# One-core decoder step: the last expert pass added through a one-hot table, row loads in freed buffers, the shared product spread over pairs

## The chip, the cores and the metric

The kernel runs on one core of a Trainium2 chip. The metric is the device time of one launch in microseconds (us). Engines are named as the profile names them: PE (matrix), DVE (vector), ACT (scalar), POOL (GpSimd) and SP (which only starts DMAs here).

## What is computed

One decoder layer for 576 tokens (512 prompt tokens, 64 sample tokens): attention and a gated convolution, a layer norm, a mixture of 64 experts, a shared expert, a per-layer embedding term, a second layer norm. What the change touches is the second half:

```python
eidx, gw = route(x2, lw['w_router'], lw['router_bias'])      # 6 of 64 experts a token
ffn = (swiglu(x2, lw['w_s_gate'], lw['w_s_up'], lw['w_s_down'])          # shared expert
       + routed_experts(x2, eidx, gw, lw['w_e_gate'], lw['w_e_up'], lw['w_e_down']))
ple = jax.nn.sigmoid(h @ lw['w_ple_gate']) * (p @ lw['w_ple_proj'])
h = layer_norm(DN_ALPHA * h + ffn.reshape(n, s, D_MODEL) + ple, lw['ln2_g'], lw['ln2_b'])
```

A token is 1024 wide, an expert's hidden width is 256, everything is float32. An expert's three matrices are 3 MB, so 64 experts are about 200 MB to be read.

## The kernel before

**Passes and pairs.** Experts are taken in 32 pairs (`pair(p, i)`). A pair's weights (six loads of 1 MB: gate, up and down of both experts) go into one of three buffers, `w_exp[RING[p % 3]]`, at the SBUF offsets `o_w0`, `o_w1` and `o_w2`. A pass computes 64 rows of each of the two experts. A pair takes as many passes as its fuller expert needs, read at run time from `n_pass`. In this input there are 40 passes; the running sum after each pair is in `cum_pass`, and if it came out odd the last pair would get an empty pass more.

**What each engine does in a pass k.** PE multiplies the turned rows `xt` by gate (`gate_mm`) and up (`gu_ready`), transposes the next pass's rows (`turn`, L1311), transposes the hidden rows, and multiplies by down (`y_mm`). ACT and DVE scale the two halves of the result by the token's weight into `ysb[:, k % 2]`. POOL gathers the rows of pass k + 2 from DRAM into `xg` (L690) and then scatters `ysb` to `expert_rows` in DRAM (L715), one row for each of a token's six choices. Both are indirect DMAs on POOL's queue; all three streams use the same 16 DMA engines.

**What SP does.** It loads pair p (`next_pair`, L569) part by part. Each part waits for the same part of pair p - 3 to have been used and for that of pair p - 1 to have landed. The weights of pair 2 and, ahead of them, the shared expert's down matrix `w_sdn` (L610) wait until PE has finished the last of 20 units of the embedding gate (`u_ready`). PE turns the rows of pass 0 just ahead of that unit.

**The shared expert's down product** (`shared_down`, `shared_add`) is ten tiles of 512 columns, put behind pairs 0, 1 and 2 as `SD_AFTER` says (4, 3 and 3 tiles). Behind each group PE waits until DVE has added the last of them.

**The last stage.** When all passes are scattered, POOL signals `all_out` and SP loads the rows back, nine loads of 1.5 MB: two for each of the four prompt tiles (`part[t]`, L623), one for the sample tile (`fold`, L625). For a prompt tile PE sums the first `N_ON_PE[t]` of the six rows through the identity matrix (L1401), DVE adds the others to `res` (`add_rows`, L1939), then the sum of PE (`add_sum`, L1955), ACT makes the variance (L970), DVE scales (`last_norm`, L1966 and L1968) and SP writes the tile out (L630). The sample tile comes last and is folded by DVE and PE.

## Time and profile before

| | |
|---|---|
| median of 3 runs | 1310.81 us (1310.05 to 1314.06) |
| time of the profiled execution | 1311.96 us |
| its span in the profile | 1310.1 us |
| PE busy | 1223.2 us, 93% of the span |
| DVE busy | 488.2 us, 37% |
| ACT, POOL busy | 304.2 us and 159.5 us |
| HBM read, written | 295.95 MB and 26.94 MB |

The profile lists when instructions ran on each engine and what the engine had waited for. DMA shares are the busy part of 16 DMA engines; they can read a little over 1. Times of single instructions are counted from the start of the span.

### The profile page before, as it was taken

How to read it: one execution, taken by the hardware profiler on the slowest of the kernel's cores; microseconds unless marked ns; L12 is line 12 of the kernel's file. 1: busy time of each engine (PE TensorE's matmuls, PEld its weight loads, DVE VectorE, ACT ScalarE, POOL GpSimd, SP SyncE). 2: the span in 40 equal slices, each digit the busy share in tenths (PEclk: the TensorE clock that was granted, in tenths of full speed). 3: DMA queues.
4: the chain of work that ended last, by engine and by line, in shares of the span. 5: the costliest groups of instructions: out<-in, count | busy, mean ns of one | idle time of the engine just before them, and what ended most of it. 6: DMA issues, size and time to landing. Idle time of an engine off the chain costs nothing.

```text
span 1310.1 us, 23451 instructions
## 1 busy us (share of the span) xinstructions
PE 1223.2 (93%) x8835; PEld 988.2 (75%) x8836; DVE 488.2 (37%) x1072; ACT 304.2 (23%) x557; POOL 159.5 (12%) x230
## 2 busy tenths in 40 slices
PE   6999999999999999999998899999998899999745
PEld 6988879999999999998996556666665566666412
DVE  4355683423344334575872221111111111111137
ACT  3254553312122223124121011111111111111102
POOL 0200000000000000006152111121121111211100
PEclk9999999999999999999999999999999999999968
DMA  9311212232323232433519998999999999999785
GB/s 270 102 33 65 65 34 65 65 97 65 97 66 98 65 114 81 153 95 126 225 47 413 420 393 328 419 421 422 420 412 411 415 413 408 415 408 418 295 318 231
DMA packets 101263, 308.08 MB, mean 235 GB/s; under 512 B 11435, under 2 KB 62467, under 8 KB 76613
## 3 DMA queue, kind: packets, MB, share of 16 engines
q1 hardware_dynamic: 87636, 275.20, 54.8%
q0 software_dynamic: 12480, 28.60, 5.7%
q10 hardware_dynamic: 1088, 3.47, 0.8%
q8 instruction: 41, 0.67, 0.2%
q14 instruction: 18, 0.14, 0.0%
HBM read 295.95 MB, written 26.94 MB: 246 GB/s over the span
## 4 chain that ended last, share of the span: by engine, by line
PE 51%; DMA 38%; DVE 5%; issue 1%; SPq 1%; DVEq 1%; ACT 1%; POOL 1%; ACTq 0%; POOLq 0%
DMA w_exp<-in_w_e_down_dram 35%; PE proj L992 31%; PE proj L1172 4%; PE att L1349 2%; PE proj L1366 2%; PE proj L1301 2%; DMA part<-expert_rows 2%; PE att L1097 1%; PE att L1059 1%; PE att L1181 1%; PE proj L1025 1%; SPq L623 1%; PE att L1172 1%; PE att L1110 1%; PE att L1381 1%
## 5 line engine op out<-in xcount | busy, mean ns | idle before, releaser
L1349 PE MATMUL att<-w_exp,xt 128*64 128x256 f32 x2560 | 288.9, 383 | 21.6 <-issue 10.0
L1349 PEld LDWEIGHTS att<-w_exp,xt 128*64 128x64 f32 x2560 | 221.1, 138 | 99.6 <-issue 46.6
L992 PE MATMUL proj<-h_hi,w_hi 128*128 128x288 f32 x768 | 171.2, 304 | 0.0
L992 PE MATMUL proj<-h_hi,w_lo 128*128 128x288 f32 x768 | 164.2, 295 | 0.0
L992 PE MATMUL proj<-h_lo,w_hi 128*128 128x288 f32 x768 | 164.0, 295 | 0.0
L1366 PE MATMUL proj<-w_exp,ht_e 128*64 128x512 f32 x640 | 147.3, 601 | 9.3 <-issue 5.2
L992 PEld LDWEIGHTS proj<-h_hi,w_hi 128*128 128x128 f32 x768 | 122.0, 189 | 16.2 <-issue 15.2
L992 PEld LDWEIGHTS proj<-h_lo,w_hi 128*128 128x128 f32 x768 | 123.6, 189 | 0.0
L992 PEld LDWEIGHTS proj<-h_hi,w_lo 128*128 128x128 f32 x768 | 123.4, 188 | 0.0
L448 DVE TENSOR_TENSOR w_lo<-w_raw,w_hi 128x2048 fp32r<-128x2048 f32 x33 | 75.6, 2290 | 94.4 <-ACT w_hi L438 88.1
L1366 PEld LDWEIGHTS proj<-w_exp,ht_e 128*64 128x64 f32 x640 | 50.5, 137 | 78.6 <-issue 75.8
L438 ACT ACTIVATE w_hi<-w_raw 128x2048 fp32r<-128x2048 f32 x33 | 63.0, 1910 | 90.6 <-PE proj L992 73.9
L1911 DVE TENSOR_SCALAR ysb<-proj,tabw 128x512 f32 x40 | 30.0, 751 | 140.3 <-PE proj L1366 140.3
L1902 DVE TENSOR_TENSOR sg<-sg,att 128x256 f32<-128x256 f32 x40 | 16.8, 421 | 127.5 <-ACT sg L947 127.5
L1906 DVE TENSOR_TENSOR h_e<-sg,att 128x256 f32<-128x256 f32 x40 | 16.8, 421 | 123.6 <-PE att L1349 123.6
L954 ACT ACTIVATE ysb<-proj,tabw 128x512 f32 x40 | 27.5, 687 | 141.8 <-PE proj L1366 141.8
L1311 PEld LDWEIGHTS proj<-ident,xg 128*128 128x128 f32 x328 | 43.5, 195 | 19.7 <-issue 15.1
L949 ACT ACTIVATE ht_e<-att 128x256 f32<-128x256 f32 x40 | 15.3, 383 | 185.3 <-PE att L1355 185.3
L1311 PE MATMUL proj<-ident,xg 128*128 128x128 f32 x328 | 54.5, 290 | 4.0 <-DMA xg<-x_rows,gidx_col 4.0
L715 POOL DMA_INDIRECT expert_rows<-ysb,sidx_col x40 | 40.4, 1010 | 137.8 <-DVE ysb L1911 133.5
L992 PE MATMUL proj<-mix_hi,w_lo 128*128 128x288 f32 x256 | 54.8, 296 | 0.0
L992 PE MATMUL proj<-mix_hi,w_hi 128*128 128x288 f32 x256 | 54.8, 296 | 0.0
(342 smaller groups left out, 1761.0 us busy)
## 6 DMA issues: line engine op xcount, KB each, us to landing
w_exp<-in_w_e_gate_dram SPq DMA_DIRECT2D x64, 1024.0 KB
w_exp<-in_w_e_up_dram SPq DMA_DIRECT2D x64, 1024.0 KB
w_exp<-in_w_e_down_dram SPq DMA_DIRECT2D x64, 1024.0 KB
w_raw<-in_w_in_dram SPq DMA_DIRECT2D x21, 1024.0 KB
part<-expert_rows SPq DMA_DIRECT2D x8, 1536.0 KB, 17.8
w_raw<-in_w_in_dram SPq DMA_DIRECT2D x8, 512.0 KB
w_raw<-in_w_attn_out_dram SPq DMA_DIRECT2D x8, 512.0 KB
w_raw<-in_w_conv_out_dram SPq DMA_DIRECT2D x4, 1024.0 KB
```

The source lines that it names most:

```text
L438: nc.scalar.activation(w_hi[:, g.par, :], w_raw[:, g.par, :], ACT.Copy).then_inc(hi_done, 1)
L448: nc.vector.tensor_tensor(w_lo[:, g.par, :], w_raw[:, g.par, :], w_hi[:, g.par, :].bitcast(F32), ALU.subtract).then_inc(w_ready, 1)
L715: pool.indirect_dma_start(out=rows_d[:, :], out_offset=bass.IndirectOffsetOnAxis(ap=sidx_col[i][:, 0:1], axis=0), in_=ysb[:, i, :], in_off ...
L954: nc.scalar.activation(ysb[:, bass.ds(side_of, 1), 0:512].rearrange("p o n -> p (o n)"), proj[:, 2, :], ACT.Copy, scale=tabw[:, bass.ds(k, ...
L992: last = nc.tensor.matmul(proj[:, 2 * i + a, 0:HALF], lhs, x[:, c, a * HALF:(a + 1) * HALF], start=(c == 0 and n == 0), stop=(c == KC - 1 ...
L1172: last = nc.tensor.matmul(out, x[:, c, t * P:t * P + w], v[:, c, :], start=(c == 0 and n == 0), stop=(c == KC - 1 and n == 2))
L1301: last = nc.tensor.matmul(gate_bank(u)[0:w, :], x[:, c, t * P:t * P + w], v[:, c, :], start=(c == 0 and n == 0), stop=(c == KC - 1 and n = ...
L1311: last = nc.tensor.transpose(proj[:, half, c * P:(c + 1) * P], xg[:, :, half * 4 + c], ident[:, :])
L1349: last = nc.tensor.matmul(att[e * SLOT:(e + 1) * SLOT, m, 0:FF], xt[:, c, e * SLOT:(e + 1) * SLOT], weights[e][:, c, :], start=(c == 0), s ...
L1366: last = nc.tensor.matmul(proj[e * SLOT:(e + 1) * SLOT, 2 + half, :], ht_e[:, c, e * SLOT:(e + 1) * SLOT], down[e][:, c, half * 512:(half ...
L1902: nc.vector.tensor_tensor(sg[:, :], sg[:, :], att[:, 0, 0:FF], ALU.mult)
L1911: nc.vector.tensor_scalar(ysb[:, bass.ds(side_of, 1), 512:D].rearrange("p o n -> p (o n)"), proj[:, 3, :], tabw[:, bass.ds(k, 1)], None, A ...
```

## The change

Five things change.

1. **Last pass.** The last pass is no longer scattered to DRAM and read back. POOL's loop makes one pass fewer (`half_all` is one lower, one `next_rows` stands behind the loop). Its results stay in `ysb[:, 1]`. ACT and DVE split them into `y_hi` and `y_lo`, and PE adds them to each token tile's sum through `slot_hot`, a table with a one where slot and token match, made by DVE behind pair 19. As its rows in `expert_rows` are still read, POOL writes zeros there from the cleared `xg`, ahead of the first gather, which waits for it.
2. **Row loads.** The row tiles now lie in the three weight buffers: four loads in `o_w2`, four in `o_w0`, one in `o_w1`. `all_out` comes when pass 38 is scattered, and SP starts each group of loads when the pair that last used the buffer is done (`pair_done`). A row tile is 3 x 1024 floats in one piece. The sample tile comes second, and PE sums its three pieces itself (`fold_rows` is gone).
3. **Shared product.** One tile behind each of pairs 5 to 14 (`SD_FIRST`, `N_SD`), in one PSUM bank. `w_sdn` is loaded behind the weights of pair 4.
4. **Gain and bias of the second norm.** ACT loads one row of each ahead of the passes, where before it loaded them spread over 128 partitions behind the passes; PE spreads them through a row of ones behind pairs 15 to 18, DVE copies them.
5. **Code.** 20 pairs are written out for PE and DVE (before 5 and 3) and the rest looped; ACT has one loop. `N_ON_PE` of tile 3 is 3 instead of 4. ACT reads its square-root table ahead of the tiles.

```diff
+SD_FIRST = 5
+N_SD = 2 * NT
+N_UNROLLED = 20
+LAST_ORDER = (0, NT - 1, *range(1, NT - 1))
-N_ON_PE = (2, 3, 4, 4)
+N_ON_PE = (2, 3, 4, 3)
...
+        o_part = [(o_w2, o_w0, o_w1)[n // 4] + n % 4 * 12 * D for n in range(9)]
...
-            sp.dma_start(w_sdn[:, :, :], w_sd[0].rearrange("(c p) n -> p c n", p=P)).then_inc(sd_in, 16)
             load_parts(2, 2, range(4))
             sp.wait_ge(res_done, 1)
             load_parts(2, 2, range(4, 6))
             for p in range(3, 5):
                 next_pair(p, RING[p % 3], p - 3)
+            sp.dma_start(w_sdn[:, :, :], w_sd[0].rearrange("(c p) n -> p c n", p=P)).then_inc(sd_in, 16)
...
             sp.wait_ge(all_out, 1)
...
+            def pair_done(p):
+
+                done = sp.value_load(cum_pass[0:1, p:p + 1], min_val=1, max_val=MAXPASS - 1)
+                sp.wait_ge(y_mm, done)
+                past(nc.sync, 4)
...
+            pair_done(NPE - 3)
+            for h in range(2):
+                load_rows(0, h)
...
+            load_rows(1, 0)
+            pair_done(NPE - 2)
+            load_rows(1, 1)
+            for h in range(2):
+                load_rows(2, h)
+            load_rows(3, 0)
+            pair_done(NPE - 1)
+            load_rows(3, 1)
...
-            gather(0, 0, 1)
+            k_half = half_passes(pool)
+            nc.gpsimd.tensor_copy(sidx_col[1][:, :], tabs[:, bass.ds(k_half * 2 + 1, 1)]).then_inc(idx_ready, 1)
+            pool.wait_ge(idx_ready, 1)
+            pool.indirect_dma_start(out=rows_d[:, :], out_offset=bass.IndirectOffsetOnAxis(ap=sidx_col[1][:, 0:1], axis=0),
+                                    in_=xg[:, :, :].rearrange("p q c -> p (q c)"), in_offset=None, bounds_check=8 * T - 1,
+                                    oob_is_err=False).then_inc(scattered, 16)
+            pool.wait_ge(scattered, 16)
+            gather(0, 0, 2)
...
             with pool.Fori(0, k_half) as it:
...
+                    next_rows(it * 2 + i, i)
+            next_rows(k_half * 2, 0)
...
+            act.wait_ge(y_a, k + 1)
+            act.wait_ge(y_dv, k + 1)
+            past(nc.scalar, 0)
+            nc.scalar.activation(y_hi[:, :], ysb[:, 1, :], ACT.Copy).then_inc(y_hi_ready, 1)
+            nc.scalar.activation(sink_s[:, :], eps[:, :], ACT.Sqrt)
...
-            for p in range(5):
+            for p in range(N_UNROLLED):
                 pair(p, RING[p % 3])
...
+                if 0 <= n < N_SD:
+                    shared_down(n)
+                if N_SD <= n < N_SD + 4:
+                    spread_row(n)
...
+            for s, t in enumerate(LAST_ORDER):
+                w = ntok(t)
+                if s == 4:
+                    pe.wait_ge(part_added, 1)
+                out = sum_banks(s)[0:w, :, :]
...
+                pe.wait_ge(y_lo_ready, 1)
                 for half in range(2):
...
+                    for n, y in enumerate((y_hi, y_lo)):
+                        last = nc.tensor.matmul(out[:, half, :], slot_hot[:, t * P:t * P + w],
+                                                y[:, half * 512:(half + 1) * 512], start=False, stop=(n == 1))
...
+            dve.wait_ge(y_hi_ready, 1)
+            dve.drain()
+            nc.vector.tensor_tensor(y_lo[:, :], ysb[:, 1, :], y_hi[:, :].bitcast(F32), ALU.subtract).then_inc(y_lo_ready, 1)
...
+            for s in range(NT + 2):
+                if s < NT and LAST_ORDER[s] < NT - 1:
+                    add_rows(LAST_ORDER[s])
+                if 1 <= s <= NT:
+                    add_sum(s - 1, LAST_ORDER[s - 1])
+                if s >= 2:
+                    last_norm(s - 2, LAST_ORDER[s - 2])
```

On POOL, at the end of the embedding units, the first gather stood like this before (`xg` are the gathered rows, `ppo` the embedding product, `xtr` PE's signal that rows are turned):

```order
L661 TENSOR_TENSOR ppo_131<-ppo_131,sig_g 64x256 [waits u_sig]
L687 COPY gidx_col_201<-tabx 128x1 [waits x_zero,x2_out,routed]
L690 DMA xg<-x_rows,gidx_col_201 128x1024 [waits idx_ready]
L661 TENSOR_TENSOR ppo_131<-ppo_131,sig_g 128x256 [waits u_sig] x4
L661 TENSOR_TENSOR ppo_131<-ppo_131,sig_g 64x256 [waits u_sig]
```

In the changed kernel the same place on POOL reads:

```order
L690 TENSOR_TENSOR ppo_131<-ppo_131,sig_g 64x256 [waits u_sig]
L474 TENSOR_LOAD half_all [waits x_zero,x2_out,routed]
L474 ISA x2
L724 ISA
L724 COPY sidx_col_204<-tabs 128x1
L726 DMA expert_rows<-xg,sidx_col_204 4608x1024 [waits idx_ready]
L716 COPY gidx_col_201<-tabx 128x1 [waits scattered]
L719 DMA xg<-x_rows,gidx_col_201 128x1024 [waits idx_ready]
L690 TENSOR_TENSOR ppo_131<-ppo_131,sig_g 128x256 [waits u_sig] x4
```

The write of zeros, and the wait for its landing, have come between the embedding products and the first gather, and the last five products stand behind both.

On SP, behind the loop over pairs, the end of the program was this:

```order
L623 DMA part_205<-expert_rows 128x3x1024 [waits all_out]
L623 DMA part_205<-expert_rows 128x3x1024
L623 DMA part_206<-expert_rows 128x3x1024 x2
L623 DMA part_207<-expert_rows 128x3x1024 x2
L623 DMA part_208<-expert_rows 128x3x1024 x2
L625 DMA fold<-expert_rows 128x3x1024
```

In the changed kernel it is this, still on SP:

```order
L635 TENSOR_LOAD cum_pass [waits all_out]
L635 ISA x2
L642 DMA part_0_205<-expert_rows 128x3072 [waits y_mm]
L642 DMA part_1_206<-expert_rows 128x3072
L648 DMA fold<-expert_rows 128x3072
L642 DMA part_0_207<-expert_rows 128x3072
...
L642 DMA part_1_208<-expert_rows 128x3072 [waits y_mm]
L642 DMA part_0_209<-expert_rows 128x3072
L642 DMA part_1_210<-expert_rows 128x3072
L642 DMA part_0_211<-expert_rows 128x3072
...
L642 DMA part_1_212<-expert_rows 128x3072 [waits y_mm]
```

There are still nine loads, and `all_out` is still ahead of them; only the last one waits for the last pair.

## Rows read from the trace of the kernel before

**Rows 1.** The page: span, and DMA busy share in 40 slices.

```profile
span 1310.1 us, 23451 instructions
DMA  9311212232323232433519998999999999999785
```

**Rows 2.** Stretches: busy us of each engine (instructions), PE clock, DMA share, GB/s.

```profile
700.00:770.00 70.00, 59.37 (x338) 33.47 (x338) 14.25 (x24) 6.53 (x13) 9.22 (x15) 0.98 1.01 414
770.00:797.60 27.60, 27.23 (x212) 18.44 (x209) 4.84 (x9) 4.48 (x9) 4.84 (x8) 1.00 0.78 303
797.60:1236.00 438.40, 417.13 (x3054) 274.07 (x3050) 77.39 (x136) 69.34 (x135) 82.70 (x136) 0.99 1.01 412
1236.00:1254.06 18.06, 8.92 (x59) 5.18 (x58) 2.28 (x4) 2.05 (x4) 2.43 (x4) 0.88 0.33 113
1254.06:1290.40 36.34, 23.06 (x42) 9.54 (x43) 19.52 (x21) 4.35 (x7) 0.00 (x0) 0.73 0.99 394
```

**Rows 3.** Timeline of PE behind pair 2: start, us, what ran [idle before].

```profile
768.54 7.13 PE L1349 MATMUL att<-w_exp,xt 128*64 128x256 f32 x64 [1.96 <-issue]
780.89 7.10 PE L1349 MATMUL att<-w_exp,xt 128*64 128x256 f32 x64
```

**Rows 4.** Instructions grouped by line, pair stage: count, busy us, mean ns.

```profile
L1381 PE MATMUL att<-w_sdn,hs_x 128*128 128x512 f32 (+1 forms) x40 | 18.1, 601 | 0.0
```

**Rows 5.** Timeline of SP: the loads around the dip in DMA.

```profile
701.57 0.38 SPq L610 DMA_DIRECT2D w_sdn<-in_w_s_down_dram  x1
781.32 0.84 SPq L569 DMA_DIRECT2D w_exp<-in_w_e_down_dram  x2
797.63 0.99 SPq L569 DMA_DIRECT2D w_exp<-in_w_e_gate_dram  x2
```

**Rows 6.** Timeline of POOL and PE: first gather; a scatter and the gather behind it.

```profile
688.10 1.35 POOL L690 DMA_INDIRECT xg<-x_rows,gidx_col  x1 [0.95 <-POOL gidx_col L687]
697.67 1.13 PE L1311 MATMUL proj<-ident,xg 128*128 128x128 f32 x8 [0.72 <-DMA xg<-x_rows,gidx_col]
...
807.80 1.00 POOL L715 DMA_INDIRECT expert_rows<-ysb,sidx_col  x1 [3.38 <-DVE ysb L1911]
...
815.54 1.04 POOL L690 DMA_INDIRECT xg<-x_rows,gidx_col  x1 [0.85 <-DMA expert_rows<-ysb,sidx_col]
```

**Rows 7.** Who waited for whom, pair stage: us in total, times, longest.

```profile
PE att L1349 <- DMA w_exp<-in_w_e_up_dram: 9.7, 5, 2.5
```

**Rows 8.** Timeline: the last two scatters, and the start of the row loads.

```profile
1232.76 1.02 POOL L715 DMA_INDIRECT expert_rows<-ysb,sidx_col  x1 [4.03 <-DVE ysb L1911]
...
1248.84 1.01 POOL L715 DMA_INDIRECT expert_rows<-ysb,sidx_col  x1 [4.04 <-DVE ysb L1911]
1254.06 15.81 SPq L623 DMA_DIRECT2D part<-expert_rows  x8
```

**Rows 9.** Timeline of DVE: rows of tiles 0 and 3 added, last instruction.

```profile
1264.13 5.13 DVE L1939 TENSOR_TENSOR res<-res,part 128x1024 f32<-128x1024 f32 x4 [16.27 <-DMA part<-expert_rows]
...
1287.03 2.53 DVE L1939 TENSOR_TENSOR res<-res,part 128x1024 f32<-128x1024 f32 x2 [0.78 <-DMA part<-expert_rows]
...
1305.50 1.28 DVE L1968 SCALAR_TENSOR_TENSOR res<-res,rstd,g2b 64x1024 f32<-64x1024 f32 x1
```

**Rows 10.** Instructions grouped by line, last stage.

```profile
L1401 PE MATMUL att<-part,ident 128*128 128x512 f32 x32 | 15.7, 654 | 2.2 <-DMA part<-expert_rows 2.2
L1939 DVE TENSOR_TENSOR res<-res,part 128x1024 f32<-128x1024 f32 x11 | 13.5, 1226 | 22.4 <-DMA part<-expert_rows 21.9
L1968 DVE SCALAR_TENSOR_TENSOR res<-res,rstd,g2b 128x1024 f32<-128x1024 f32 (+1 forms) x5 | 6.4, 1283 | 0.4
L1966 DVE SCALAR_TENSOR_TENSOR res<-res,mv,g2b 128x1024 f32<-128x1024 f32 (+1 forms) x5 | 6.3, 1263 | 0.0
```

**Rows 11.** Single microseconds of the last stage, columns as in Rows 2.

```profile
1250.00:1251.00 1.00, 0.00 (x0) 0.00 (x0) 0.00 (x0) 0.00 (x0) 0.00 (x0) 0.50 0.94 258
1282.00:1283.00 1.00, 1.00 (x3) 0.41 (x2) 0.89 (x2) 0.00 (x0) 0.00 (x0) 0.50 1.03 418
```

More of the change, by code:

```diff
@@ L1386, in _, with shared_down, spread_row @@
-            for p in range(5):
+            def shared_down(n):
+                t, c = QUADS[n]
+                w = ntok(t)
+                pe.wait_ge(sd_read, n)
+                for k in range(2):
+                    last = nc.tensor.matmul(sd_bank(n)[0:w, :], hs_x[:, k, t * P:t * P + w],
+                                            w_sdn[:, k, c * 512:(c + 1) * 512], start=(k == 0), stop=(k == 1))
+                last.then_inc(sd_ready, 1)
+            def spread_row(n):
+                i, c = divmod(n - N_SD, 2)
+                pe.wait_ge(sd_read, n)
+                nc.tensor.matmul(sd_bank(n), ones_row[:, :], g2b2[0:1, i, c * 512:(c + 1) * 512],
+                                 start=True, stop=True).then_inc(sd_ready, 1)
@@ new lines, in _ @@
+            with pe.Fori(0, (NPE - N_UNROLLED) // 3) as it:
+                for i in range(3):
+                    pair(it * 3 + (N_UNROLLED + i), RING[(N_UNROLLED + i) % 3])
+            k = pe.snap(count, min_val=0, max_val=MAXPASS - 2)
+            pe.wait_ge(y_a, k + 1)
+            pe.wait_ge(y_dv, k + 1)
+            past(nc.tensor, 1)
+            pe.wait_ge(hot_ready, 1)
+            for s, t in enumerate(LAST_ORDER):
+                w = ntok(t)
+                if s == 4:
+                    pe.wait_ge(part_added, 1)
+                out = sum_banks(s)[0:w, :, :]
+                if t == NT - 1:
+                    pe.wait_ge(part_in[t], 16)
+                    for half in range(2):
+                        for j in range(TOPK // 2):
+                            nc.tensor.matmul(out[:, half, :], fold_id[:, :], fold[:, j, half * 512:(half + 1) * 512],
+                                             start=(j == 0), stop=False)
+                else:
+                    pe.wait_ge(part_in[t], 32)
+                    for half in range(2):
+                        for j in range(N_ON_PE[t]):
+                            nc.tensor.matmul(out[:, half, :], ident[:, :], part_row(t, j, half), start=(j == 0), stop=False)
+                pe.wait_ge(y_lo_ready, 1)
@@ L1403, in _ @@
                 last.then_inc(part_sum, 1)
-            pe.wait_ge(folded, 1)
-            pe.wait_ge(part_added, 1)
-            for half in range(2):
-                last = nc.tensor.matmul(sum_banks(NT - 1)[0:NS, half, :], fold_id[:, :],
-                                        fold[:, 0, half * 512:(half + 1) * 512], start=True, stop=True)
-            last.then_inc(part_sum, 1)
         @block.vector
@@ L1934, in add_rows @@
+            dve.drain().then_inc(hot_ready, 1)
+            with dve.Fori(0, NPE - N_UNROLLED) as it:
+                passes(it + N_UNROLLED)
+            dve.wait_ge(y_hi_ready, 1)
+            dve.drain()
+            nc.vector.tensor_tensor(y_lo[:, :], ysb[:, 1, :], y_hi[:, :].bitcast(F32), ALU.subtract).then_inc(y_lo_ready, 1)
             def add_rows(t):
```

187 lines of the change are left out of this document (86 added, 101 removed).

## The prediction, made blind

> **What bounds the kernel now.** I read the page first: from about 690 us on, the DMA share is nine tenths or more in nearly every slice [rows 1]. That is the pair stage, 200 MB of weights. A table of stretches then says where the transfers stand still. Between 700 and 770 us and again from 797.6 to 1236 us the share is 1.01, which is as full as this trace reads [rows 2]. It drops twice: to 0.78 in the 27.6 us from 770 on, and to 0.33 in the 18 us between the last weights and the first row load [rows 2]. From 1254.06 on it is full again with the row loads, and then a tail of DVE and output follows to the end.
>
> So two kinds of time can be gained: idle DMA inside the pair stage, and time around its end. PE work in the pair stage is worth something only where it keeps a buffer from coming free.
>
> The first dip is such a place. SP issues the down part of one pair at 781.32 and the next gate part at 797.63 [rows 5]: it waits for a buffer. PE runs its passes back to back there, 12.35 us apart (768.54 and 780.89) [rows 3], and it is late because of the shared product: 18.1 us of matmuls [rows 4], and behind each of the three groups a gap of 1.9 to 2.0 us in which PE waits for DVE (one of the three: [rows 3]). Between two pairs without a shared group there is no gap [rows 3]. Later PE waits for weights: 9.7 us for up parts alone, five times [rows 7].
>
> **1. Start of the pair stage: a loss.** Before, POOL issued the first gather at 688.10, and PE, which waited for it, turned the rows at 697.67: 9.6 us, beside weight loads that fill the queues [rows 6]. Now POOL first loads a register, copies an index, writes the zeros and waits until they have landed, and the gather queues behind all that. PE's last gate unit stands behind the turn, SP's loads of pair 2 behind that unit, and with them every later load.
> - The register load has no row of its own. The 1.96 us gap contains one, beside other work [rows 3], so it costs 0 to 2 us; I take 1.0.
> - An indirect write in a full queue: issued at 807.80, and the gather of 815.54, which had 0.85 us of idle before it, is put down to its landing [rows 6]. So it landed 6.9 to 7.7 us after its issue; I take 7.3. Below, the last scatter, in a nearly empty queue, took at most 5.2 us to the row loads (1248.84 to 1254.06) [rows 8]. Above, 9.6 as the gather.
> - Index copy and its wait again: 1.3 us (0.95 of it the wait) [rows 6].
> - The gather now runs while the queue drains: between 5.2 (as above) and 9.6; I take 7.0.
>
> Sum 1.0 + 7.3 + 1.3 + 7.0 = 16.6 against 9.6: PE's turn and SP's loads come 7.0 us later. Bounds: with 5.2 twice and no register load +2.1, with 9.6 twice and 2 us +12.9.
>
> The Trainium skill (DMA: Bandwidth & Descriptors, section Anatomy of one DMA) fits a POOL-issued DMA with 2.0 us plus its bytes at 436 GB/s. By it each of the two 0.5 MB transfers would take 3.2 us (an estimate), the start would be about 1 us earlier than before, and the sum below 1290.5. The trace disagrees while SP's queue is full: 9.6 us for the gather.
>
> **2. The dip: a gain.** PE reaches pair 3 earlier by 18.1 us and three gaps of 1.9, together 23.8, less the 7.0. The gate part of 797.63 could then be issued some 17 us earlier, and the dip is only (1.01 - 0.78) / 1.01 x 27.6 = 6.3 us of idle DMA, so all of it goes. In exchange the queue is empty for the 7.0 us at the start. `w_sdn` is only moved. The zeros are new traffic: 0.5 MB at 0.414 MB/us is 1.3 us at most. The longer code for PE (15 more pairs written out) adds bytes I take as nothing.
>
> Last weights: +7.0 - 6.3 + 1.3 = 2.0 us later. Bounds: -3 and +8.
>
> PE must not become the bound instead. The ten tiles come back behind pairs 5 to 14 (18.1 us), and four spread rows of at most half a tile each (0.9) make 3.6. So by pair 18 PE stands at +7.0 - 23.8 + 18.1 + 3.6 = 5 us later than before, and it has 9.7 us of waits for weights to give there [rows 7]. Hidden. DVE's table behind pair 19 (some 12 small instructions) lies in DVE's idle time: DVE is busy 77 of 438 us [rows 2].
>
> **3. The row loads: the main gain.** `all_out` now needs the scatter of pass 38, issued at 1232.76, instead of that of pass 39, issued at 1248.84 [rows 8]. From there to SP's first load it took 5.2 us before; weights still land until about 1236 [rows 2], so I take 6.0, and 1.0 for SP's register load. With the 2.0 us of part 2: 1232.8 + 2.0 + 6.0 + 1.0 = 1241.8, which is 12.3 us ahead of 1254.06. The buffers are no limit: eight of the nine loads need pairs 29 and 30, whose last pass is 38, and the ninth pair 31, done before its turn in the queue comes.
>
> The loads themselves take as long as before. The first two land 10.1 us after the first issue (1254.06 to 1264.13), the eighth 33.0 us after (1287.03) [rows 8, 9]: 3.8 us each. The order is tile 0, samples, 1, 2, 3, so tile 3 is complete with the ninth load, 10.1 + 7 x 3.8 = 36.7 us after the issue: 1278.5. Pieces of 12 KB instead of 4 KB I count as nothing: the share is already 0.99 [rows 2].
>
> **4. The end behind the last rows.** DVE has, behind tile 3's rows: three adds (1.23 each and their drains, 3.8), the sum of tile 2 (1.22 and two small ones, 1.4), the norm of tile 1 (1.26 + 1.28 + 0.2 = 2.7), the sum of tile 3 (1.4), the norms of tiles 2 and 3 (5.5) (means of each line: [rows 10]): 14.8 us, to 1293.3. The output took 1310.1 - 1306.8 = 3.3 us behind DVE's last instruction [rows 9, 1]. That gives a span of 1296.6.
>
> Does PE keep up? A tile is six matmuls of two records, 12 x 0.43 = 5.2 us at the full clock (15.7 us for 32 records, low stretch included, is 0.49 [rows 10]), and four one-hot matmuls, at most one record each, 1 to 2 us: 6.2 to 7.2 against 7.6 us of loading. Tile 2 has eight, and ends about 1279.5, tile 3 about 1285.5; DVE asks for it at 1286.5. So PE is hidden by 1 us. `y_hi` and `y_lo`, one instruction each of about the 1.23 us of a row add [rows 10], are made while the first rows are on their way.
>
> Other edits count as nothing: the two 0.5 MB loads of gain and bias ran while SP waited; the table load of ACT lay behind tile 0, not at the end.
>
> **Sum.** Span 1310.1 - 13.5 = 1296.6; the profiled execution's time was 1311.96, so 1298.5 by its own. That execution lies 1.2 us above the median of the three runs, 1310.81, from which the same sum gives 1297.3. I say 1298.
>
> **Rivals.**
> - *Start hidden.* Both indirect transfers take 5.2 us and the register load nothing: a delay of 2.1, the last weights 2.9 us sooner than before and 4.9 sooner than in my sum: 1293. For it: without pair 2's loads the queue runs dry while the gather is under way. Against: 9.6 us measured in that very place [rows 6].
> - *Start dear.* Both transfers take 9.6 us: the delay is 12.9 instead of 7, and the last weights come 7.9 us late: 1304.
> - *Clock.* PE rests about 4 us between the last pass and the first rows. Before, it stood at 0.50 at 1250, in the rest behind the last pass, and again at 1282, while PE worked (one microsecond of each: [rows 11]). A low stretch of 4 us costs 2 us of work. One is nearly hidden; three in tiles 1 to 3 put PE 4 to 6 us behind: 1303.
> - *Rows not earlier.* If the scatter of pass 38 lands only behind all queued weights and its last gather, SP starts at 1249 or later: gain under 5 us before part 2 and 1307 with it. Against: scatters landed in 7 us in full queues.
> - *Slower.* PE's code for pairs 5 to 19 is now fetched once for each pair, in full queues, instead of standing in a loop. If each such pair made PE wait for its code, PE would bound the stage. It has about 5 us to give (9.7 less 5), and 13.5 are gained elsewhere, so it decides from 18.5 us, 1.2 us for each of 15 pairs; at 2 us each the time is 1298 + 25 = 1323. Against: pairs 3 and 4 were already written out, and PE had no gap between them [rows 3]. The Trainium skill (Runtime: NRT & Kernel Launch, section Instruction fetch mechanics) says that a taken branch to code outside the current window stalls until a DMA has brought it; each pair here has a loop of its own. The trace shows no such stall at pairs 3 and 4.
>
> **How the numbers follow.** The forecast, with a range of its own from 1294 to 1302, gets 0.62; start hidden 0.10; start dear 0.09; clock 0.06; rows not earlier 0.06; slower 0.07. The range from 1290 to 1305 holds the first four less their edges. A change under 0.3% (4 us) is not told from none here. Faster by more (under 1306.9) are the first four and a little of the fifth: 0.88. Within it, the rest of the fifth and mild code stalls: 0.06. Slower 0.06.
>
> **What would show it.** Part 1: the turn of the first rows near 704.7 instead of 697.67, the load of pair 2 near 708.6, and DMA idle just before. Part 2: no wait of SP near 797, share 1.0 from there, pass 38's scatter 2 us later than 1232.76. PE matmuls of `w_sdn` behind pairs 5 to 14 with no gap behind them. Part 3: first row load at 1241.8. Part 4: DVE adding tile 3's rows at 1278.5 without a wait for PE behind it. The prediction fails if the pair stage ends more than 8 us late, or if PE, not the loads, paces the tiles.

## The result, and the profile after

Seven runs of the changed kernel have a median of 1305.11 us (1302.84 to 1307.29); the kernel before, run beside it, has 1313.18. One of the seven runs of the kernel before took 2456.76 us and is left out of the ratio, which is 0.9945, with a 95% interval from 0.9929 to 0.9961: faster by 7 us (5 to 9). The forecast of 1298 expected 13 us, and its range from 1290 to 1305 ended 0.1 us short of the median. In a later round the changed kernel gave 0.9940 [0.9924, 0.9956] (r12_after_again, below).

The profiled execution took 1302.84 us, and is the fastest of its seven.

The start of the pair stage, in the timelines of POOL, ACT, PE and SP (start, us, what ran, idle before and what ended it); it answers to [rows 5, 6]:

```profile
689.25 3.03 POOL L726 DMA_INDIRECT expert_rows<-xg,sidx_col  x1 [0.89 <-POOL sidx_col L724]
700.35 0.18 POOL L716 COPY gidx_col<-tabx 128x1 uint32<-128x1 uint32 x1 [8.07 <-DMA expert_rows<-xg,sidx_col]
701.42 1.07 POOL L719 DMA_INDIRECT xg<-x_rows,gidx_col  x1 [0.89 <-POOL gidx_col L716]
...
703.33 0.38 ACT L964 ACTIVATE sig_g<-proj 128x256 f32<-128x256 f32 x1 [11.21 <-POOL ppo L690]
...
705.95 1.95 PE L1356 MATMUL proj<-ident,xg 128*128 128x128 f32 x8 [8.49 <-DMA xg<-x_rows,gidx_col]
...
712.29 0.80 SPq L581 DMA_DIRECT2D w_exp<-in_w_e_gate_dram  x2
```

The zero write landed 11 us after its issue, and PE turned the first rows at 705.95 instead of 697.67. SP's first load of pair 2 came at 712.29 instead of 701.99. The turn took 1.95 us where it took 1.13 before. The table of stretches shows why, in its third column from the right (granted clock), and what the transfers did, in the second from the right (DMA share); it answers to [rows 2]. The first line is the kernel before at its turn, the others are the changed kernel:

```profile
695.00:700.00 5.00, 4.28 (x37) 4.11 (x36) 1.45 (x3) 0.98 (x2) 1.03 (x2) 1.00 1.01 424
...
700.00:705.00 5.00, 0.00 (x0) 0.00 (x0) 1.73 (x3) 0.77 (x2) 3.74 (x6) 0.60 0.88 364
705.00:710.00 5.00, 4.05 (x19) 4.08 (x20) 1.96 (x4) 0.60 (x1) 0.65 (x1) 0.50 0.01 5
710.00:770.00 60.00, 56.39 (x415) 38.49 (x415) 9.75 (x19) 8.98 (x18) 11.64 (x19) 0.96 0.96 391
770.00:797.60 27.60, 27.23 (x208) 18.13 (x204) 4.94 (x9) 4.11 (x8) 4.88 (x8) 1.00 1.02 420
797.60:1236.00 438.40, 419.81 (x2955) 256.17 (x2954) 86.42 (x156) 67.40 (x131) 79.41 (x131) 1.00 1.01 413
```

PE's clock was at half while it turned the rows and ran the last gate unit, behind 8.5 us without work; before, it was full there. For five microseconds nearly nothing was transferred (0.01). The dip from 770 on is gone: 1.02 instead of 0.78. PE's timeline shows a tile of the shared product between two pairs; the gap that stood behind a group of them in [rows 3] is gone:

```profile
799.38 3.65 PE L1411 MATMUL proj<-w_exp,ht_e 128*64 128x512 f32 x15
802.96 1.98 PE L1424 MATMUL att<-w_sdn,hs_x 128*128 128x512 f32 x4
804.87 1.51 PE L1394 MATMUL att<-w_exp,xt 128*64 128x256 f32 x11
```

The end: the scatter of pass 38, the first row load, the rows of tiles 0, 1, 2 and 3 added by DVE, and DVE's last instruction, which answer to [rows 8, 9]:

```profile
1236.52 1.02 POOL L750 DMA_INDIRECT expert_rows<-ysb,sidx_col  x1 [3.67 <-DVE ysb L1981]
...
1245.49 0.81 SPq L642 DMA_DIRECT2D part<-expert_rows  x2
...
1255.11 5.12 DVE L2034 TENSOR_TENSOR res<-res,part 128x1024 f32<-128x1024 f32 x4 [1.01 <-DMA part<-expert_rows]
1266.63 3.83 DVE L2034 TENSOR_TENSOR res<-res,part 128x1024 f32<-128x1024 f32 x3 [2.53 <-DMA part<-expert_rows]
1275.12 2.53 DVE L2034 TENSOR_TENSOR res<-res,part 128x1024 f32<-128x1024 f32 x2 [0.46 <-DMA part<-expert_rows]
1282.91 3.83 DVE L2034 TENSOR_TENSOR res<-res,part 128x1024 f32<-128x1024 f32 x3 [1.08 <-DMA part<-expert_rows]
...
1296.67 1.28 DVE L2055 SCALAR_TENSOR_TENSOR res<-res,rstd,g2b 128x1024 f32<-128x1024 f32 x1
```

```profile
span 1301.0 us, 23460 instructions
```

Pass 38's scatter is 3.8 us later than before, the first row load 8.6 us earlier, DVE starts tile 3's rows 4.1 us earlier, and the span is 9.1 us shorter. In the 9 us between scatter and first row load the transfers ran at a third of their share, in the table of stretches:

```profile
1236.00:1245.49 9.49, 8.39 (x71) 6.24 (x72) 0.84 (x2) 0.38 (x1) 1.02 (x1) 1.00 0.37 152
```

### The profile page after: what moved, and what is told of

The parts are those of the page before. It is cut to its first block, busy times and chain, and to the rows that moved or that the text cites. A ratio compares the mean times of both kernels' runs of the same rounds, so it can differ in the third digit from the quotient of the medians.

```text
span 1301.0 us, 23460 instructions
## 1 busy us (share of the span) xinstructions
PE 1232.8 (95%) x8867; PEld 983.0 (76%) x8868; DVE 493.2 (38%) x1087; ACT 305.7 (23%) x559; POOL 160.0 (12%) x227
## 4 chain that ended last, share of the span: by engine, by line
PE 47%; DMA 45%; DVE 5%; issue 1%; DVEq 1%; ACT 1%; POOL 1%; SPq 0%; ACTq 0%; POOLq 0%
DMA w_exp<-in_w_e_down_dram 41%; PE proj L1037 31%; PE proj L1217 4%; DMA part<-expert_rows 2%; PE proj L1346 2%; PE att L1142 1%; PE att L1104 1%; PE att L1226 1%; PE proj L1070 1%; DMA expert_rows<-xg,sidx_col 1%; PE att L1217 1%; PE att L1155 1%; PE proj L1330 1%; PE proj L1282 1%; DMA ident<-in_const_dram 0%
## 5 line engine op out<-in xcount | busy, mean ns | idle before, releaser
L1394 PEld LDWEIGHTS att<-w_exp,xt 128*64 128x64 f32 x2560 | 209.6, 137 | 100.8 <-issue 39.1
L1037 PE MATMUL proj<-mix_lo,w_hi 128*128 128x288 f32 x256 | 54.8, 296 | 0.0
```

The costliest lines, as they stand in the source:

```text
L1037: last = nc.tensor.matmul(proj[:, 2 * i + a, 0:HALF], lhs, x[:, c, a * HALF:(a + 1) * HALF], start=(c == 0 and n == 0), stop=(c == KC - 1 ...
L1394: last = nc.tensor.matmul(att[e * SLOT:(e + 1) * SLOT, m, 0:FF], xt[:, c, e * SLOT:(e + 1) * SLOT], weights[e][:, c, :], start=(c == 0), s ...
```

## The experiments

All ratios are against the kernel before, run on the same chip in the same rounds, and are not always the ratio of the medians; the intervals are 0.0012 to 0.0021 (2 to 3 us) to either side. "Free source" below is the version of the second experiment.

### 1. The zero write alone, on the kernel before (e1_zero_on_before)

```diff
-            gather(0, 0, 1)
+            k_half = half_passes(pool)
+            nc.gpsimd.tensor_copy(sidx_col[1][:, :], tabs[:, bass.ds(k_half * 2 - 1, 1)]).then_inc(idx_ready, 1)
+            pool.wait_ge(idx_ready, 1)
+            pool.indirect_dma_start(out=rows_d[:, :], ..., in_=xg[...]).then_inc(scattered, 16)
+            pool.wait_ge(scattered, 16)
+            gather(0, 0, 2)
```

> Edit: the kernel before, with the zero write of the changed kernel alone, issued and waited for ahead of the first gather (the dummy row write that filled its count is left out). It computes what the kernel before computes. Theory A (the wait for the zero write holds the turn, the turn holds PE and the last gate unit, these hold SP's loads of pair 2, and an idle microsecond of the DMA engines there is never won back): the first pass starts 8 to 11 us later and the time rises by 7 to 11 us, 0.5 to 0.85 %. Rival B (the late start is taken up again, since the pair stage has slack after it): the first pass starts as late, but the time rises by less than 4 us. Rival C (the dip behind the shared product is what the delay eats, because the weights of pairs 3 and 4 are only wanted later): the dip at 770 to 798 is filled and the time rises by 0 to 3 us.

Measured: 1324.97 us against 1313.49, ratio 1.0091 [1.0076, 1.0107]. That is 11.5 us, at the upper edge of theory A; B and C are out. The share from 770 to 798 is 0.99 here, but the dip is not filled: it has moved behind 800, as the stretch from 800 to 900 shows (the kernel before first, then this run):

```profile
800.00:900.00 100.00, 97.83 (x729) 65.00 (x725) 18.70 (x33) 16.41 (x32) 19.46 (x32) 1.00 1.02 420
800.00:900.00 100.00, 97.83 (x731) 64.95 (x727) 18.29 (x32) 16.41 (x32) 19.45 (x32) 1.00 0.96 394
```

0.06 x 100 is 6 us, the dip's size in [rows 2]. The delay shifted the dip and came on top of it.

### 2. Zeros from a free slot, nobody waits (e2_free_source)

```diff
+            gather(0, 0, 1)
+            nc.gpsimd.memset(ysb[:, 1, :], 0.0).then_inc(x_zero, 1)
             k_half = half_passes(pool)
-            nc.gpsimd.tensor_copy(sidx_col[1][:, :], tabs[:, bass.ds(k_half * 2 + 1, 1)]).then_inc(idx_ready, 1)
-            pool.wait_ge(idx_ready, 1)
-            pool.indirect_dma_start(out=rows_d[:, :], ..., in_=xg[...]).then_inc(scattered, 16)
-            pool.wait_ge(scattered, 16)
-            gather(0, 0, 2)
...
-            gather(1, 1, 3)
+            gather(1, 1, 2)
+            pool.wait_ge(x_zero, 2)
+            nc.gpsimd.tensor_copy(sidx_col[1][:, :], tabs[:, bass.ds(k_half * 2 + 1, 1)]).then_inc(idx_ready, 1)
+            pool.wait_ge(idx_ready, 3)
+            pool.indirect_dma_start(out=rows_d[:, :], ..., in_=ysb[:, 1, :]).then_inc(scattered, 16)
```

> Edit: the changed kernel with the zeros of the last pass's rows taken from a slot of the output buffer that is free then (POOL sets it to zero behind the first gather), so that the first gather goes first and the zero write goes behind the second gather with nothing waiting for it at the start. Theory A: PE's turn returns from 706 to 697 to 699 us, the clock does not fall there, the pair stage ends 8 to 11 us earlier, and the time is 0.992 to 0.994 of the changed kernel's, about 1295 us. Rival B: start 8 us earlier, end the same within 3 us.

Measured: 1295.69 us, 0.9867 [0.9852, 0.9882]; once more, as r14_free_again, 1295.33 us, 0.9860 [0.9846, 0.9874]. This beats both kernels: 18 us under the kernel before, and 9.4 us under the changed one by medians. The clock is full while PE turns the rows (699.87) and runs the last gate unit, and the DMA share stays near 1:

```profile
700.00:710.00 10.00, 8.11 (x74) 7.03 (x76) 1.83 (x5) 1.36 (x3) 3.58 (x6) 1.00 0.98 389
710.00:720.00 10.00, 7.65 (x46) 4.45 (x44) 1.28 (x3) 0.98 (x2) 1.43 (x3) 0.83 1.02 414
```

### 3. The turn behind the last gate unit (e3_turn_late)

```diff
-            turn(0)
             gate_unit(N_BLK * NT - 1)
+            turn(0)
```

> Edit: the changed kernel with PE's turn of the first rows behind the last gate unit instead of ahead of it, so that SP, which waits for the last gate unit, may load pair 2 some 9 us earlier, while the zero write, its wait and the first gather stay as they are. The first pass starts as late as in the changed kernel or 1 us later. Theory A1 (what the late start costs is the idle time of the DMA engines): the DMA engines are busy from 703 us on, the pair stage ends 6 to 9 us earlier, the time falls by 6 to 9 us, to 0.993 to 0.995 of the changed kernel's. Rival B1 (what it costs is that the passes start late and PE is never done earlier): the time stays within 2 us.

Measured: 1300.84 us, 0.9909 [0.9894, 0.9925]: 4.3 us under the changed kernel, about half of A1. The timelines of PE and ACT show why only half:

```profile
706.64 0.45 PE L1346 MATMUL proj<-pg_hi,xt_hi 128*64 128x256 f32 x1 [4.63 <-ACT sig_g L964]
```

```profile
706.11 0.38 ACT L964 ACTIVATE sig_g<-proj 128x256 f32<-128x256 f32 x1 [9.44 <-POOL ppo L690]
```

The last gate unit did not wait for the turn now, but for a sigmoid, which waited 9.4 us for a product of POOL, which stood behind the wait for the zero write. A second chain led from that wait to SP's loads. The prediction had only the one through the turn.

### 4. Both chains cut, first pass still late (e8_loads_on_time)

```diff
+            for u in range(3 * NT, N_BLK * NT - 1):
+                ple_product(u)
             pool.wait_ge(scattered, 16)
             gather(0, 0, 2)
-            for u in range(3 * NT, N_BLK * NT):
-                ple_product(u)
+            ple_product(N_BLK * NT - 1)
```

and PE's two lines as in experiment 3.

> Edit: the changed kernel with the turn of the first rows behind the last gate unit on PE, and POOL's products of the units 15 to 18 ahead of the wait for the zero write's landing instead of behind it, so that neither path holds the last gate unit, for which SP's loads of pair 2 wait. The first pass starts as late as in the changed kernel. Theory A1 (the price of the late start is idle time of the DMA engines): SP's loads go 8 to 9 us earlier and the time falls by 7 to 9 us, to 0.988 to 0.989 of the kernel before, as with the zero write moved away altogether. Rival B1 (half of the price is the late first pass itself): the time falls by 3 to 5 us, 0.990 to 0.992, no more than with the turn moved alone.

Measured: 1295.63 us, 0.9872 [0.9857, 0.9888], the same as the free source. SP's loads went at 700.10, while the first rows were turned at 708.19, even later than in the changed kernel:

```profile
700.10 0.80 SPq L581 DMA_DIRECT2D w_exp<-in_w_e_gate_dram  x2
```

```profile
708.19 1.97 PE L1357 MATMUL proj<-ident,xg 128*128 128x128 f32 x8 [8.13 <-DMA xg<-x_rows,gidx_col]
```

The table of stretches:

```profile
700.00:710.00 10.00, 1.87 (x9) 1.57 (x8) 0.00 (x0) 0.00 (x0) 0.69 (x1) 0.70 1.02 428
710.00:720.00 10.00, 7.66 (x47) 4.95 (x48) 2.00 (x5) 1.24 (x3) 1.92 (x3) 0.62 1.02 405
```

PE was busy 1.9 of the first ten microseconds and its clock was lower than in the changed kernel's second ten (0.62 against 0.77), and none of this cost time that could be measured. So the price of the start is the idle time of the DMA engines, within the 2 us of the intervals.

### 5. The write ahead, without its wait (e5_no_wait)

```diff
+            nc.gpsimd.memset(ysb[:, 1, :], 0.0).then_inc(x_zero, 1)
...
-                                    in_=xg[:, :, :].rearrange("p q c -> p (q c)"), in_offset=None, bounds_check=8 * T - 1,
+                                    in_=ysb[:, 1, :], in_offset=None, bounds_check=8 * T - 1,
...
-            pool.wait_ge(scattered, 16)
             gather(0, 0, 2)
```

> Edit: the changed kernel with the zero write still ahead of the first gather, but taken from the free slot of the output buffer (set to zero by POOL first), so that the gather follows at once and nothing waits for the write to land at the start. It splits the price of the zero write into its issue with the packets ahead of the gather's, and the wait for its landing. If the wait is what costs (theory A), the time is that of the version with the write behind the second gather plus 2 to 4 us (setting the slot to zero, index copy, issue), 0.988 to 0.990 of the kernel before. If the write's packets hold up the gather's in the queue, it stays within 3 us of the changed kernel, 0.993 to 0.995.

Measured: 1302.05 us, 0.9920 [0.9906, 0.9933]: 3 us under the changed kernel, and between the two expectations. The gather, issued at 692.37, 3.1 us behind the write, was there for PE at 703.03, 10.7 us later. So of the 9.4 us only a third is the wait; two thirds remain. Counted from the last product of POOL ahead of this place, SP's first load of pair 2 goes 7.2 us later than with the free source. 4.1 us of that is POOL's work ahead of the gather's issue (clearing the slot, register, index, the write's issue of 2.0 us); the gather then takes 1.2 us longer, 10.7 instead of 9.5, and the way from the turn to SP's load 2.0 us longer. The last is the clock, which fell here as well, behind 5.9 us of rest of PE:

```profile
700.00:710.00 10.00, 5.85 (x32) 5.62 (x32) 1.02 (x2) 0.97 (x2) 0.63 (x1) 0.66 0.46 175
```

### 6. PE kept busy while it waits (e7_warm, e9_warm_short)

```diff
+            for _ in range(64):
+                nc.tensor.matmul(att[:, 3, 0:P], ident[:, :], ident[:, :], start=True, stop=True)
             turn(0)
```

The second run has 34 in the place of 64.

> Edit: the changed kernel with 64 matmuls of a constant matrix, results unused, on PE ahead of the turn of the first rows (some 7 of the 8.5 us that PE waits there), so that PE is busy while it waits; all else as changed. Theory A (2 to 2.5 us of the late start are the granted clock, which fell to 0.50 while PE waited): the turn takes 1.1 us instead of 1.95, the last gate unit returns to full speed, and the time falls by 1.5 to 3 us, 0.9923 to 0.9935 of the kernel before. Rival B: the clock is full and the time stays within 1 us, since the rest of the chain waits for something else (POOL's products, which are queued behind the wait for the zero write).

Measured: 1307.65 us, 0.9955 [0.9942, 0.9969]: slower than the changed kernel by 1 to 3 us, which neither theory had. The added work was too long: 0.226 us for each matmul, 14.5 us in all, and it kept PE from rows that could have been there some 5.6 us earlier (an estimate from the changed kernel's 4.5 us for the gather). What the run does show is the clock. PE's turn and SP's load:

```profile
715.93 1.04 PE L1356 MATMUL proj<-ident,xg 128*128 128x128 f32 x8
```

```profile
719.74 0.80 SPq L581 DMA_DIRECT2D w_exp<-in_w_e_gate_dram  x2
```

From turn to load it is 3.8 us at the full clock, where the changed kernel takes 6.3 (705.95 to 712.29).

> Edit: the changed kernel with 34 matmuls of a constant matrix on PE ahead of the turn of the first rows, where the run with 64 had them; those took 14.5 us, 0.226 us each, and were 5.6 us too long, so 34 last 7.7 of the 8.5 us that PE waits. Theory A (the granted clock behind PE's wait is 2.5 us of the late start, and SP's loads come as much earlier): from the turn's start to SP's first load of pair 2 3.8 us instead of 6.3, and the time 2 to 3 us below the changed kernel's, 0.992 to 0.993 of the kernel before. Rival B (the price of the start is not in the clock): within 1 us of the changed kernel, 0.994 to 0.995.

Measured: 1302.05 us, 0.9911 [0.9893, 0.9928], against 0.9940 of the changed kernel beside it: 2.7 us less by medians, as theory A has it. Its profiled execution doesn't show it, though: it is one of the slower ones of its runs (1303.74), the rows came 2.0 us behind the end of the added work, SP's first load of pair 2 was no earlier (712.90), and the clock fell even so:

```profile
708.00:710.00 2.00, 2.00 (x13) 2.00 (x13) 1.02 (x2) 0.60 (x1) 0.00 (x0) 0.59 0.00 0
```

So the size of the clock's term, 2.5 us, is read from e7_warm; that it is worth as much in the time is suggested by the medians of e9_warm_short and not shown by its trace.

### 7. The shared product undone, and alone (e4_shared_back, e6_spread_alone)

Undone on the changed kernel:

```diff
             sp.wait_ge(u_ready, N_BLK * NT)
+            sp.dma_start(w_sdn[:, :, :], ...)
             load_parts(2, 2, range(4))
...
+                if p < 3:
+                    shared_down(SD_AFTER[p])
-                if 0 <= n < N_SD:
-                    shared_down(n)
```

> Edit: the changed kernel with the shared product back in three groups of four, three and three tiles behind pairs 0, 1 and 2 (with the wait for the tiles' readers behind each group) and its weights loaded ahead of pair 2, the rest as changed. Theory A: the DMA dip returns (a share near 0.78 at 770 to 798, some 6 us of idle time) and the time rises by 3 to 7 us, 0.2 to 0.5 %. Rival B (the dip was slack already, since the DMA queue had run ahead): the dip returns and the time stays within 2 us.

Measured: 1309.72 us, 0.9971 [0.9958, 0.9983]: 4.6 us more by medians. The dip is back, partly behind 800, since the first passes are late:

```profile
770.00:800.00 30.00, 27.72 (x174) 16.38 (x170) 5.50 (x9) 3.12 (x6) 3.50 (x6) 0.94 0.92 367
800.00:900.00 100.00, 97.56 (x726) 64.99 (x724) 18.62 (x33) 16.41 (x32) 19.45 (x32) 1.00 0.96 392
```

0.08 x 30 and 0.04 x 100 are 6.4 us of idle transfers; against the changed kernel's 1.02 and 1.01 it is 8 us, for 4.6 us of time. The opposite edit, the shared product's part alone on the kernel before (loads of `w_sdn` behind pair 4, one tile behind each of pairs 5 to 14):

> Edit: the kernel before with the shared product alone changed (its weights loaded behind pair 4, one tile behind each of pairs 5 to 14, pairs 0 to 16 written out). It computes what the kernel before computes. Theory A (the three parts add up, and the shared product's part is worth 3.5 to 5 us as its undoing on the changed kernel showed): 0.9960 to 0.9975 of the kernel before. Rival B (on the kernel before, the start of the pair stage is not late, so the queue has run ahead and the dip costs less): within 2 us, 0.9985 to 1.0.

Measured: 1304.92 us, 0.9937 [0.9924, 0.9951]: 8 us (6 to 10), more than either theory had, and not the 2 us of B. The share from 770 to 800 is 1.01:

```profile
770.00:800.00 30.00, 29.25 (x208) 18.20 (x206) 6.01 (x10) 4.79 (x9) 6.20 (x11) 1.00 1.01 419
```

### 8. The last pass's part alone (e10_last_alone)

The edits of experiments 2 and 7 (undone) together.

> Edit: the last pass and the row loads as changed, zeros from the free slot behind the second gather, and the shared product as in the kernel before. It is the last pass's part without the two others. Theory A (parts add up): 13 to 15 us below the kernel before, 0.9885 to 0.990. Rival B (the last pass's part is worth what is left between the shared product alone and the version with both and the free source, some 9 us): 0.9925 to 0.994, and then the version with both gains more than the sum.

Measured: 1300.03 us, 0.9910 [0.9888, 0.9931]: 12 us (9 to 15) under the kernel before, between A and B; the interval reaches into both. Its dip stands where it stood:

```profile
770.00:800.00 30.00, 29.63 (x233) 20.36 (x231) 4.99 (x9) 4.49 (x9) 4.88 (x8) 1.00 0.81 318
```

The free source with the shared product spread is 4.3 to 5.0 thousandths lower, 6 us. Undone on the changed kernel it was worth 4.6, alone 8. The intervals are 2 us to either side of each, and one value of 6 us, the idle time of the dip, lies within or at the edge of all three. Whether it differs between them is not settled, and neither is why it should.

### 9. Row loads 15 us earlier, and 5 us later (e11_other_rows, e13_rows_later, r14_free_again)

Both are edits of the free source:

```diff
-            sp.wait_ge(all_out, 1)
+            other_d = w_eg[0].rearrange("e (q r) n -> (e q) (r n)", r=4)
...
-                rows = rows_d[t * P * 8:(t + 1) * P * 8, :].rearrange("(p h i) n -> p h i n", h=2, i=4)
+                rows = other_d[t * P * 8:(t + 1) * P * 8, :].rearrange("(p h i) n -> p h i n", h=2, i=4)
```

and the same for the samples' rows; the second edit is

```diff
-            pair_done(NPE - 3)
+            pair_done(NPE - 1)
             for h in range(2):
                 load_rows(0, h)
```

> Edit: the version with the zeros from the free slot, and the row loads of the end taken from another tensor in DRAM of the same size, so that they wait only for the weights' buffers and not for the last scatter; it leaves out reading the experts' rows. Theory A (SP's wait for the last scatter, 9 us in which the DMA engines are three quarters idle, and the 5 us ahead of it hold the whole end back one to one): the first row load goes at 1226 to 1233 instead of 1239, tile 3 is complete 8 to 14 us earlier, and the time falls by 8 to 13 us, to 0.977 to 0.981 of the kernel before. Rival B (the loads of the last tiles wait for pair 39's buffer or DVE is busy with the last passes, so that an earlier start of the loads is eaten up): less than 5 us, 0.983 to 0.987.

Measured: 1293.31 us, 0.9856 [0.9838, 0.9875]: only 1 to 2 us under the free source. SP's first row load went at 1223.25 instead of the free source's 1238.77, and theory A fell. The stretches show what took over; behind the length (10.00) the first number is PE's busy time, the third DVE's:

```profile
1250.00:1260.00 10.00, 10.00 (x28) 4.04 (x27) 5.30 (x7) 1.53 (x3) 0.00 (x0) 1.00 1.01 426
1260.00:1270.00 10.00, 10.00 (x26) 4.74 (x25) 9.34 (x15) 2.84 (x6) 0.00 (x0) 1.00 0.47 198
```

The rows of tile 3 were added at 1271.22 with no wait for a transfer, and PE was busy without a rest from 1250 to 1270:

```profile
1271.22 3.82 DVE L2035 TENSOR_TENSOR res<-res,part 128x1024 f32<-128x1024 f32 x3
```

They were added 4 us earlier than in r14_free_again below (1275.17), for row loads that went 14 to 15 us earlier.

> Edit: the version with the zeros from the free slot, with SP's first row load waiting for the last pass's down product as well as for the last scatter. That product ends some 6 us behind the landing of the last scatter, so that all nine row loads go 5 to 6 us later and nothing else moves. It gives the slope on the late side: theory A (the row loads set the end one to one as long as they are no earlier than in the changed kernel, so the 2.0 us by which the landing of the last scatter was longer than forecast are 2.0 us of the end): 4 to 6 us above its neighbour without the wait. Rival B (PE's sums and DVE's chain set the end already, as they do where the row loads go 15 us earlier, so the landing's 2 us cost nothing): 0 to 2 us above it.

> The version with the zeros from the free slot once more, as the neighbour of the run with later row loads. Both theories: 0.985 to 0.989 of the kernel before.

Measured: 1300.66 us, 0.9908 [0.9893, 0.9924], against 1295.33, 0.9860, beside it. First row load and tile 3's rows, with the later load first:

```profile
1242.56 0.82 SPq L642 DMA_DIRECT2D part<-expert_rows  x2
...
1280.11 3.83 DVE L2035 TENSOR_TENSOR res<-res,part 128x1024 f32<-128x1024 f32 x3 [0.33 <-DMA part<-expert_rows]
```

```profile
1237.66 0.81 SPq L642 DMA_DIRECT2D part<-expert_rows  x2
...
1275.17 3.82 DVE L2035 TENSOR_TENSOR res<-res,part 128x1024 f32<-128x1024 f32 x3 [1.05 <-DMA part<-expert_rows]
```

Loads 4.9 us later, tile 3's rows 4.9 us later, time 5.3 us more: one to one, as theory A has it. So the row loads set the end from the free source's place on towards later, and the changed kernel's first row load (1245.49) is later still; its trace has DVE wait 1.08 us for the rows of tile 3. Somewhere within the 15 us ahead of the free source's place PE and DVE take over.

### 10. The changed kernel once more (r12_after_again)

> The changed kernel once more, beside the three others. Both theories: 0.993 to 0.996 of the kernel before; its profile shows how far the stretch at the start of the pair stage differs from one execution to the next.

Measured: 1304.71 us, 0.9940 [0.9924, 0.9956]. SP's first load of pair 2 is at 712.02 in its profile and the scatter of pass 38 at 1236.03, within 0.5 us of the first one: the late start is no accident of one execution.

## Why the prediction was wrong

The chain of the prediction is the one that came: a late start, the dip gone, earlier row loads, the tail behind tile 3. Two steps of its sum failed. Step 1 took the way from the turn to SP's loads as it was before and had no term for the low clock there; step 3 took the landing of pass 38's scatter from the wrong scatter. A smaller term, the row loads themselves, was 0.7 us short, and the base was low.

**Step 1, the start: +7.0 forecast, 8.9 to 10.7 measured.** The 8.9 us are the DMA idle time below, the 10.7 us SP's first load behind the last gate unit (701.57 to 712.29), of which 0.5 us was there before POOL reached this place. PE's turn was forecast at 704.7 and came at 705.95. That this was near is luck: the write took 11.0 us from issue to landing, not 7.3, and the gather 4.5 us, not 7.0, each outside its own bounds (at most 9.6, at least 5.2), to opposite sides. The 7.3 was no landing that the row shows. The prediction took the 0.85 us ahead of the gather of 815.54 for a wait for the scatter, but in the code a gather waits for its index only, and the same idle time stands ahead of the others:

```profile
716.31 1.02 POOL L690 DMA_INDIRECT xg<-x_rows,gidx_col  x1 [0.85 <-POOL gidx_col L687]
```

The larger part of the error was made behind the turn. The sum took the way from there to SP's loads as it was before, 3.9 to 4.3 us (697.67 to 701.57 and 701.99). It took 6.3, because the clock was at half: in e7_warm, at the full clock, it took 3.8. The prediction had the clock as a rival for the last stage only and not here, though its own sum let PE stand waiting for the rows some 7 us longer. The second chain through POOL's products was missed too; it is hidden behind the first, and shows when the first is cut.

How much DMA idle time costs can be read over the experiments. Idle is (1 - share) x 30 us, from 687 to 717 us of each profile. The profiled executions of e1, e3 and e7 reach this place 4.3 to 4.6 us later than the changed kernel's (SP's last load of pair 1 at 694.4 to 694.7 instead of 690.1), so they are read from 691.5 to 721.5. The extra time is that of the medians, against the free source's 1295.69 (e1: against the kernel before).

| run | DMA share | DMA idle, us | extra time, us |
|---|---|---|---|
| e8_loads_on_time | 1.00 | 0 | -0.1 |
| e3_turn_late | 0.86 | 4.2 | 5.2 |
| e5_no_wait | 0.81 | 5.7 | 6.4 |
| e1_zero_on_before | 0.71 | 8.7 | 11.5 |
| the changed kernel | 0.70 | 9.0 | 9.4 |
| e9_warm_short | 0.69 | 9.3 | 6.4 |
| e7_warm | 0.61 | 11.7 | 12.0 |

Five of the seven lie within 1 us of one to one. e1 is 2.8 us above it and e9 2.9 us below, with intervals of 2 us and one profiled execution for each; so the slope is near one, and not known closer than that. In stretches of ten the changed kernel has shares of 1.02, 0.45 and 0.66 from 690 to 720: 5.5 + 3.4 = 8.9. The rival "start hidden" is out, and "start dear" (12.9) was nearer for the write and wrong for the gather.

**Step 2, the dip: right.** 6.3 us of idle time were forecast to go, and the share of the stretch went from 0.78 to 1.02; undone or done alone the part is worth 4.6 to 8 us. The last weights were forecast 2.0 us later, and pass 38's scatter came 3.8 us later: 8.9 - 6.3 + 1.3 = 3.9. The error is that of step 1, carried on. The code of 15 more pairs written out cost nothing that can be seen: there is no gap in front of the next pair in the rows above, from 803 to 1213 us no rest of PE that is not a wait for weights or DVE is longer than 0.2 us, and e6_spread_alone, with 17 pairs written out, is 8 us faster. The Trainium skill (Runtime: NRT & Kernel Launch, section Instruction fetch mechanics) has a taken branch stall when its target is outside the fetched window; no such stall shows in this trace at pairs 5 to 19, and whether a branch there leaves that window no run shows.

**Step 3, the row loads: 12.3 us earlier forecast, 8.6 measured.** Of the 3.7 us missing, 1.8 is the end of step 2. The other 2.0 is the term of 6.0 from the scatter's issue to its landing, with 1.0 for SP's register: 9.0 instead of 7.0 (1236.52 to 1245.49), 8.2 of it the landing. The prediction had sized it by the last scatter, pass 39's, of at most 5.2 us. That one is the exception: the median from issue to landing in the pair stage of the changed kernel is

```profile
expert_rows<-ysb,sidx_col POOLq DMA_INDIRECT x39, 8.5
```

and in the trace of the kernel before, pass 38's own scatter, issued at 1232.76, had its last packets on POOL's queue between 1240 and 1241, some 8 us later. Experiment 9 shows that a later row load reaches the end one to one. The loads themselves took 37.4 us to tile 3 instead of 36.7. Alone, the part was worth 12 us (9 to 15) where the sum had 14.2 (13.5 + 7.0 - 6.3).

**Step 4, the tail: right.** 14.8 us from tile 3's rows to DVE's end were forecast, and 1282.91 + 14.8 + 3.3 is 1301.0, the span. PE was hidden, as forecast; experiment 9 shows it as a bound beside DVE once the loads are much earlier.

**The sum.** 1.8 (last weights) + 2.0 (landing) + 0.7 (loads) = 4.5, against 1301.0 - 1296.6 = 4.4 us of span. Of the other 2.7 us of 1305.1 - 1298, 2.4 is no mechanism: the forecast stood on three runs with a median of 1310.81, and the kernel before has since given 1312.8 to 1313.5 in rounds of 7 to 12 runs. Against those the sum of the runs is -12 (last pass) - 6 (shared product) + 10 (zero write) = -8, and 7 to 8 were measured. The zero write, a mere 0.5 MB, took back about half of the 18 us that the other parts brought.

## What to carry to other kernels

Where transfers bound a stage, price a delay at its start as idle time of the DMA engines: here PE could be 8 us late and at half clock for nothing, as long as the loads were issued on time. An idle stretch that vanishes from one place may only have moved; look at the stretch behind it. Size a transfer by its own kind in its own place (here 39 scatters with a median of 8.5 us), not by the one that happens to stand nearest. Look for every chain from a new wait to the queue that issues the loads, the work queued behind the wait on its own engine too, and reckon the work behind a long wait at the low clock. A wait for a buffer's old content is often avoided by another source (here a slot that is free at that moment: 9.4 us for one memset of 1 us).

## What was not expected of the hardware

- An indirect write of 0.5 MB landed 11.0 us after its issue behind full queues, and its issue kept POOL 3.03 us where others took 1.0. In e3 and e8 the same write was issued in 1.08 us and had landed after at most 9.3 and 9.4 us; what makes the difference is open. The gather behind it, in an idle queue, took 4.5 us, where it took 9.6 beside the weights [rows 6]. The Trainium skill (DMA: Bandwidth & Descriptors, section Anatomy of one DMA) gives 2.0 us and the bytes at 436 GB/s, an estimate of 3.2 us for each; the 4.5 us of that gather are the nearest to it here.
- The scatter of pass 38 took 8.2 us with the transfers at a share of 0.37, about the median of 8.5 us of all 39, most of them in full queues, and that of pass 39 in the kernel before at most 5.2 us, with a share of 0.94 at 1250 [rows 8, 11]. POOL's queue moved 0.43 MB in each case. Beside pass 38's scatter the last weights were still under way: PE waited for the last down part until 1246.87 in the changed kernel, and until 1243.14 in the kernel before, where the prediction had them land by about 1236. Beside pass 39's there were none. Whether that is the reason is open; no experiment here was made for it.
- In the changed kernel, the run without the wait and e8, the clock stood at half behind 5.9 to 8.5 us of rest of PE, in e3 at 0.51 from 705 to 710 behind 4.6 us, and in e9 at 0.59 from 708 to 710 behind 2.0 us; in the kernel before, with 0.7 us of rest in the same place, it was full.
